# Weight sums of the layer 1 projection made one stage earlier, its products, slots and queues put in another order

## What is computed

```
z = h_lat @ w_in                               # 1024 x 1024 by 1024 x 2560
q = z[..., :o1]; k = z[..., o1:o2]; v = z[..., o2:o3]; g = z[..., o3:]
q = axial_rope(q, cos_r, sin_r, cos_c, sin_c)  # x*cos + swapped(x)*sin
k = axial_rope(k, cos_r, sin_r, cos_c, sin_c)
zc = h_ctx @ w_in[:, o1:o3]                    # context tokens: keys and values only
...                                            # windowed attention over q, k, v
y_lat = (o * jax.nn.silu(g)) @ w_out
```

## Time and profile before

| what | value |
|---|---|
| median of 3 runs | 1467.51 us |
| profiled execution, its own time | 1465.17 us |
| its span, first to last instruction | 1463.3 us |
| mean granted PE clock | 0.973 of full |
| PE busy | 1356.0 us (93%) |
| DVE busy | 974.8 us (67%) |
| ACT busy | 764.6 us (52%) |
| POOL busy | 558.1 us (38%) |
| layer 1's pairs, first to last matmul | 900.03 to 1126.56 us |

### The profile page before, as it was taken

The page is one execution under the profiler, slowest core; times in us unless marked ns, Lnnn a source line. Parts: engine busy times, 40 slices in busy tenths (PEclk is TensorE's granted clock), DMA queues, the critical chain, the costliest instruction groups (busy, mean ns, idle before and its releaser), DMA issues. The chain is left out here.

```text
span 1463.3 us, 20257 instructions
## 1 busy us (share of the span) xinstructions
PE 1356.0 (93%) x7116; PEld 1147.2 (78%) x7116; DVE 974.8 (67%) x1380; ACT 764.6 (52%) x1230; POOL 558.1 (38%) x297
## 2 busy tenths in 40 slices
PE   5999999999999999999999999578966899998898
PEld 4788888888888888878888887466755788887786
DVE  7788878777787878832111556777532899997742
ACT  5474838374656556832222434232421899997521
POOL 0024131322222323114434345576410666666642
PEclk9999999999999999999999999789987999999999
DMA  9413122212122222544344444434374744233683
GB/s 376 157 59 127 66 91 77 93 63 93 63 93 74 86 100 64 214 151 143 115 129 155 147 166 133 133 108 121 110 184 130 208 129 110 79 94 101 201 253 121
DMA packets 100894, 187.21 MB, mean 128 GB/s; under 512 B 11072, under 2 KB 59744, under 8 KB 98528
## 3 DMA queue, kind: packets, MB, share of 16 engines
q1 hardware_dynamic: 100832, 186.41, 39.8%
HBM read 137.08 MB, written 49.30 MB: 127 GB/s over the span
## 5 line engine op out<-in xcount | busy, mean ns | idle before, releaser
L1061 PE MATMUL slab<-h_hi,w_hi 128*128 128x512 f32 x720 | 256.3, 356 | 3.4 <-DVE h_lo L400 2.6
L1062 PE MATMUL slab<-h_lo,w_hi 128*128 128x512 f32 x720 | 255.6, 355 | 0.0
L1063 PE MATMUL slab<-h_hi,w_lo 128*128 128x512 f32 x720 | 255.1, 354 | 0.0
L1033 POOL TENSOR_TENSOR w_lo<-wraw,w_hi 128x1024 fp32r<-128x1024 f32 x29 | 78.5, 2706 | 300.5 <-ACT w_hi L653 300.5
L2792 POOL TENSOR_TENSOR probs<-probs,rdenom 128x2560 f32<-128x2560 f32 (+1 forms) x32 | 135.7, 4242 | 52.9 <-DVE rdenom L2740 52.9
L1061 PEld LDWEIGHTS slab<-h_hi,w_hi 128*128 128x128 f32 x720 | 136.5, 190 | 23.3 <-DVE h_lo L400 2.9
L1063 PEld LDWEIGHTS slab<-h_hi,w_lo 128*128 128x128 f32 x720 | 136.3, 189 | 19.2
L1062 PEld LDWEIGHTS slab<-h_lo,w_hi 128*128 128x128 f32 x720 | 136.5, 190 | 18.9
L2761 DVE TENSOR_TENSOR pt_lo<-TB,pt_hi 128x512 fp32r<-128x512 f32 x152 | 103.9, 687 | 26.9 <-ACT pt_hi L2700 24.7
L2732 DVE CUSTOM_DVE_ANT_0 probs<-S,mask,nsink 128x640 f32<-128x640 f32 (+1 forms) x128 | 107.6, 843 | 2.5 <-PE S L2823 2.3
L2661 ACT ACTIVATE probs<-probs,neg_max 128x640 f32<-128x640 f32 (+1 forms) x128 | 102.7, 802 | 11.9 <-DVE neg_max L2732 9.3
(11 more groups left out here) (409 smaller groups left out, 3584.2 us busy)
## 6 DMA issues: line engine op xcount, KB each, us to landing
wraw<-in_w_in SPq DMA_DIRECT2D x32, 512.0 KB, 3.5
wm<-in_wm SPq DMA_DIRECT2D x32, 512.0 KB, 3.7
mixT<-work SPq DMA_DIRECT2D x16, 640.0 KB, 4.0
wm<-in_wm SPq DMA_DIRECT2D x8, 1024.0 KB, 17.0
mraw<-mixT SPq DMA_DIRECT2D x16, 512.0 KB, 6.3
q_parts<-qT SPq DMA_DIRECT2D x32, 256.0 KB, 5.0
oT<-o_out SPq DMA_DIRECT2D x8, 1024.0 KB, 6.9
work<-in_xT SPq DMA_DIRECT2D x8, 640.0 KB, 8.4
```

Source lines behind the costliest of these rows:

```text
L1033: sub(w_lo[:, j % 2].rearrange("p k n -> p (k n)"), wraw[:, j % 2, :], v32(w_hi[:, j % 2].rearrange("p k n -> p (k n)")), ALU.subtract).th ...
L1061: nc.tensor.matmul(out, l_hi, r_hi, start=start, stop=False)
L1062: nc.tensor.matmul(out, l_hi, r_lo, start=False, stop=False)
L1063: return nc.tensor.matmul(out, l_lo, r_hi, start=False, stop=stop)
```

## The change

The weight sums leave the pairs. `weight_sums(n)` on DVE makes the four sums of pair n during tile n of layer 0's output projection: SP loads the pair's two slabs to `early` (`load_pair`, which waits until the sums of the pair before are stored), DVE runs four instructions of 128x512, and SP stores two slabs of sums to a new DRAM tensor `w_sum` (`store_sums`). The first loads of layer 1 now wait until the last sums have landed. Inside the pairs, SP loads the sums ready made: `load_s34` and `load_s21` (128x1024 each), `load_x` as before (A11, A12), `load_a22` half a slab. From pair 2 on they have four slots.

POOL keeps the sine products and nothing else: the token sums (16 instructions of 128x512) and the low parts of rotated keys and queries go to DVE. The product with the cosines is written to PSUM (`VP`) and no longer to SBUF, and so is the tanh of the gates. Query results have 8 slots, `q_hi` and `q_lo` 4 each; gate results have 8 slots (`RG` and `gates`).

PE's order is S1, S2, A12, S3, S4 of a pair, then A11 of the next, then A22 of this one. The other queues follow: the copies, rotations and stores of a pair's last halves come in the next pair's turn. Attention's load of the second query block waits for the even gate pairs' stores.

```diff
         w_hi, w_lo, c1 = laid_over(nc, ("w1_hi", [P, 2, KT, P], F32R), ("w1_lo", [P, 2, KT, P], F32R),
                                    ("h1_c1", [P, 2, 2, KH, 512], F32R))
-        wb4, wb6, wb5, C, Z, R4 = laid_over(
+        wb4, wb6, wb5, Z, RQ = laid_over(
             nc, ("w1_s3", block, F32R), ("w1_a22", block, F32R), ("w1_s4", block, F32R),
-            ("rope_cosined", [P, 2, 512], F32), ("rope_swap", [P, 2, 512], F32), ("q_halves", [P, 4, 512], F32))
+            ("rope_swap", [P, 2, 512], F32), ("q_halves", [P, 8, 512], F32))
...
-        _, TG = laid_over(nc, ("over_kv_rows_too", [P, 2 * T], F32), ("g_tanh", [P, 2, 512], F32))
+        _, wraw3, wraw2, _, RG = laid_over(
+            nc, ("below_first_q", [P, 256], F32), ("w1_raw3", [P, 512], F32), ("w1_raw2", [P, D], F32),
+            ("over_first_q", [P, 512], F32), ("g_halves", [P, 4, 512], F32))
         sb("over_gw_end_too", [P, 256])
...
+
+        def load_pair(n):
+            if isinstance(n, int) and n == 0:
+                low_ready(sp, K2 - 3)
+                low_ready(sp, K2 - 2)
+            else:
+                sp.wait_ge(wss.sem, wss.at + 32 * n)
+            for i in range(2):
+                sp.dma_start(early[:, i, :], a["w_in1"][2 * n + 4 + i]).then_inc(wsr.sem, 16)
+
+        def store_sums(n):
+            sp.wait_ge(ws.sem, ws.at + 4 * n + 4)
+            for i in range(2):
+                sp.dma_start(a["w_sum"][n, i], early[:, i + 1, :]).then_inc(wss.sem, 16)
 
         def load_w(i):
...
+                store_sums(KT - 1)
+                sp.wait_ge(wss.sem, wss.at + 32 * KT)
                 first_loads()
             load_x(t)
             if not (isinstance(t, int) and t >= TT - 2):
                 load_mix(t + 2, 0)
                 load_mix(t + 2, 1)
+            if not (isinstance(t, int) and t >= KT):
+                store_sums(t - 1)
+                load_pair(t)
             store(t - 1, 1 - s)
 
...
+        def weight_sums(n):
+            x1_, x2_ = early[:, 0, 0:512], early[:, 0, 512:D]
+            y1_, y2_ = early[:, 1, 0:512], early[:, 1, 512:D]
+            dve.wait_ge(wsr.sem, wsr.at + 32 * n + 32)
+            if isinstance(n, int) and n == 0:
+                low_ready(dve, K2 - 1)
+            tt(early[:, 2, 0:512], x1_, y1_, ALU.subtract).then_inc(ws.sem, 1)
+            dve.wait_ge(ws.sem, ws.at + 4 * n + 1)
+            tt(y1_, y2_, early[:, 2, 0:512], ALU.subtract).then_inc(ws.sem, 1)
+            dve.wait_ge(ws.sem, ws.at + 4 * n + 2)
+            tt(y2_, y1_, x1_, ALU.add).then_inc(ws.sem, 1)
+            tt(early[:, 2, 512:D], x2_, y1_, ALU.subtract).then_inc(ws.sem, 1)
+
         def body(t, s, last):
             if not last:
-                epilogue(t - 1, 1 - s)
+                if isinstance(t, int) and t < 4:
+                    epilogue(t - 1, 1 - s)
+                    weight_sums(t - 1)
+                else:
+                    weight_sums(t - 1)
+                    epilogue(t - 1, 1 - s)
...
+    def raw_block(p, i):
+
+        slot, part = {A11: (0, 0), A12: (0, 1), S2: (1, 0), S1: (1, 1), S3: (2 if p > 1 else 0, 0), S4: (2 if p > 1 else 0, 1), A22: (3 if p > 1 else 1, 0)}[i]
+        return wraw[slot][:, part * 512:part * 512 + 512].rearrange("p (k n) -> p k n", n=P)
 
     def banks(p):
...
     def result(k):
 
-        return home1.R4[:, k % 4, :] if k < 4 * Q_PAIRS else gates[:, k % 4, :]
+        if k < 4 * Q_PAIRS:
+            return home1.RQ[:, k % 8, :]
+        return (home1.RG[:], gates)[k // 4 % 2][:, k % 4, :]
 
     def rotated(n):
 
         if n < 2:
             return R_kv[n][:, 0:N_LAT], CK[:], ZK[:], cos, sin
         p, m, t = half_of(n - 2)
-        return result(n - 2), C[:, n % 2, :], Z[:, n % 2, :], cos[:, t * 512:(t + 1) * 512], sin[:, t * 512:(t + 1) * 512]
+        return result(n - 2), VP[:, n % 2, :], Z[:, n % 2, :], cos[:, t * 512:(t + 1) * 512], sin[:, t * 512:(t + 1) * 512]
...
+                sp.wait_ge(bl.sem, bl.at + place(p, A12))
+                sp.dma_start(wraw[0], a["w_sum"][p, 1]).then_inc(w_ld[0], 16)
+            else:
+                if p == 2:
+                    sp.wait_ge(kst.sem, kst.at + 64)
+                else:
+                    sp.wait_ge(bl.sem, bl.at + place(p - 1, S4))
+                sp.dma_start(wraw[2], a["w_sum"][p, 1]).then_inc(sums_ld.sem, 16)
+
+        def load_s21(p):
             if p == 0:
                 sp.wait_ge(wl[1].sem, wl[1].at + 2)
             else:
-                sp.wait_ge(bl.sem, bl.at + 7 * (p - 1) + A22 + 1)
-            sp.dma_start(wraw[1], a["w_in1"][5 + 2 * p]).then_inc(w_ld[1], 16)
+                sp.wait_ge(bl.sem, bl.at + place(p - 1, S2 if p > 2 else A22))
+            sp.dma_start(wraw[1], a["w_sum"][p, 0]).then_inc(w_ld[1], 16)
+
+        def load_a22(p):
+            if p < 2:
+                sp.wait_ge(bl.sem, bl.at + place(p, S2))
+                sp.dma_start(wraw[1][:, 0:512], a["w_in1"][5 + 2 * p, :, 512:D]).then_inc(w_ld[1], 16)
+            else:
+                if p == 2:
+                    sp.wait_ge(kst.sem, kst.at + 64)
+                else:
+                    sp.wait_ge(bl.sem, bl.at + place(p - 1, A22))
+                sp.dma_start(wraw[3], a["w_in1"][5 + 2 * p, :, 512:D]).then_inc(a22_ld.sem, 16)
 
         def store_v(n):
...
+        def take(k):
             p, j = k // 4, k % 4
-            act.wait_ge(pp.sem, pp.at + 7 * p + product)
+            act.wait_ge(pp.sem, pp.at + place(p, (A11, S1, S2, A22)[j]))
             if p < Q_PAIRS:
-                if p > 0:
-                    act.wait_ge(rl.sem, rl.at + k - 1)
+                if k >= 8:
+                    act.wait_ge(rl.sem, rl.at + k - 5)
             elif p == Q_PAIRS:
-                if j == 0:
-                    act.wait_ge(rs.sem, rs.at + 2 + 4 * Q_PAIRS)
-                    act.wait_ge(rc.sem, rc.at + 2 + 4 * Q_PAIRS)
+                act.wait_ge(kst.sem, kst.at + 64)
+            elif p == Q_PAIRS + 1:
+                act.wait_ge(rs.sem, rs.at + 2 + 4 * Q_PAIRS)
+                act.wait_ge(rc.sem, rc.at + 2 + 4 * Q_PAIRS)
             else:
-                act.wait_ge(gst[j // 2], 32 * (p - Q_PAIRS))
-            nc.scalar.activation(result(k), banks(p)[bank], ACT.Copy).then_inc(cp.sem, 1)
+                act.wait_ge(gst[p % 2], 64)
...
+        def add_product(k):
+            p, j = k // 4, k % 4
+            dve.wait_ge(pp.sem, pp.at + place(p, (A12, S3, S4)[j]))
+            dve.wait_ge(cp.sem, cp.at + copied(k))
+            tt(result(k), result(k), banks(p)[(2, 0, 1)[j]], ALU.add).then_inc(cs.sem, 1)
...
-            sines(0)
-            rotated_lo(0)
-            sines(1)
-            for p in range(PAIRS):
-                more = p + 1 < PAIRS
-                k = 4 * p
-                if p > 0:
-                    half_sines(k - 1)
-                    half_lo(k - 2)
-                    half_lo(k - 1)
-                if more:
-                    third_sum(p + 1)
-                if p == 0:
-                    second_sum(1)
-                    rotated_lo(1)
-                half_sines(k)
-                if more:
-                    if p > 0:
-                        second_sum(p + 1)
-                    first_sum(p + 1)
-                    fourth_sum(p + 1)
-                half_lo(k)
-                half_sines(k + 1)
-                half_sines(k + 2)
-                half_lo(k + 1)
+            for n in range(2 + 4 * Q_PAIRS):
+                sines(n)
 
         return split, rest
 
...
+        half(0, A11)
         for p in range(PAIRS):
-            for i in (A11, A12, S2, S1, S3, S4, A22):
+            if p > 0:
+                half(p - 1, A22)
+            for i in (S1, S2, A12, S3, S4):
                 half(p, i)
+            if p + 1 < PAIRS:
+                half(p + 1, A11)
+        half(PAIRS - 1, A22)
 
```

More of the change, by code:

```diff
@@ L1741, in projections1 @@
     Q_PAIRS = KT // 2
-    A11, A12, S2, S1, S3, S4, A22 = range(7)
+    A11, S1, S2, A12, S3, S4, A22 = range(7)
     HALVES = [(0, 0), (1, 1), (0, 1), (1, 0)]
     T_TILES = (2, 3, 0, 1)
-    KD_AT, QB_AT = 5, 6
+    T_ORDER = [0, 1, 2, 4, 5, 6, 3, *range(7, 16)]
     def kv_count(s, c):
@@ L1923, in rest @@
             load_x(0)
-            load_y(0)
+            load_s21(0)
             for n in range(4):
@@ L2074, in rest @@
             evict(1, 0)
-            for n in range(3):
+            for n in (0, 1, 2, 4, 5, 6):
                 t_hi(n)
@@ L2082, in rest @@
             value_hi(1)
+            block_hi(0, A11)
             evict(2, 2)
@@ L2085, in rest @@
             value_hi(3)
-            block_hi(0, A11)
-            block_hi(0, A12)
-            for n in range(3, 7):
-                t_hi(n)
+            t_hi(3)
             value_hi(4)
             t_hi(7)
-            block_hi(0, S2)
             evict(2, 0)
@@ L2105, in rest @@
             evict(3, 1)
-            block_hi(0, A22)
             for p in range(PAIRS):
@@ L2244, in rest @@
                 k = 4 * p
```

(25 more changed lines are left out.)

402 lines of the change are left out of this document (212 added, 190 removed).

## The result

| | before | after |
|---|---|---|
| median of the runs | 1467.45 us (4 runs, 1465.69 to 1468.35) | 1422.64 us (4 runs, 1420.79 to 1424.49) |
| ratio | | 0.9696, 95% interval 0.9679 to 0.9713 |
| profiled execution, its span | 1465.17, 1463.3 us | 1424.49, 1422.7 us |
| output projection, from its third tile to the first key product | 182.3 us | 201.9 us |
| first key product to first pair product | 62.7 us | 58.6 us |

The change makes the kernel 44.8 us faster. The forecast was 65, so the measured time lies above the forecast range. The pair stage came out nearly as worked out; the output projection of layer 0, which was priced at nothing, became 20 us longer.

The account below looks back on a forecast made before the run. Bound: layer 1's pairs, query pairs by a chain over POOL, gate pairs by result slots. 154.5 + 2 + 4.2 + 2 + 1.7 = 164.4 us for a stage of 229.7, so 1399.9 profiled, 1402 us median; range 1391 to 1419.

Parts of the forecast that it names:

- Sums in the output projection: Layer 0's output projection: the added DVE sums, loads and stores fit into free time, so they cost 0.
- Rival 4: Output projection: SP's round trip of the sums ahead of the `x1` store lengthens eight turns; 1470 us, chance 2%.
- Layer 1's first loads, "hidden": End of the output projection: these loads wait some 6 us for the last sums to land, hidden; uncovered 6 us.
- 56 products at full clock, 154.5 us: Layer 1's pair stage: PE must do 56 block products of 2.76 us each, 154.5 us.
- Query pairs: Layer 1's pairs 1 to 3: DVE sets 20.7 us a pair, 1.4 over PE's 19.3; 4.2 us (0 to 8).
- rival 1: Pairs 1 to 3: DVE's chain of waits, not its sum, sets 24 us a pair; +15, 1417 us, chance 14%.
- above 23 us: Sign in layer 1's pairs: the prediction is wrong if query pairs stay above 23 us.
- Gate pairs: Layer 1's gate pairs: with more result slots PE should run; gaps of 0.5 us a pair, 2 us (0 to 10).
- if ACT still waits for `sgT`: Sign in layer 1's gate pairs: the prediction is wrong if ACT still waits for `sgT` stores to land.
- Product order and lag: Layer 1's pairs: each PSUM bank gets at least one product, 2.76 us, before reuse; four waits a pair become none.
- Start-up: Pairs 0 and 1, which share slots and get sums late: 2 us (0 to 8), replacing gaps of 3.16 and 16.63.
- DVE with PSUM: Cosine product and tanh writing PSUM: 0 added per instruction, up to 0.9 us possible, four times a pair.

## Why the prediction was wrong, step by step

On the profiled execution the forecast was 1399.9 us and 1424.5 was measured, 24.6 more. The first pair product came at 917.1 and not at 896.9 (+20.2), the pair stage took 167.8 and not 164.4 (+3.4), and what follows 1.1 more.

*Sums in the output projection: the step that failed.* It compared SP's wait for "a landing of 6.3" with 14 us free ahead of the `x1` store, summed DVE's work against DVE's idle time, and came to "Price 0". Both sums were right as sums: the runs with the DMAs alone and with DVE's work alone cost 1 and 0 to 3 us, and DVE's work beside POOL took 7.4 us a turn where 7 was worked out. What it left out is that the two are joined. `weight_sums` is an instruction of DVE's fixed order with a wait in it, for a load that waits for a store that waits for the sums before; and from turn 4 the normalisation of the finished tile is queued behind it. The landing that counts is not one but two (8.7 and 6.7 us), and what waits for them is not only the `x1` store but everything on DVE. The question what is queued behind the waiting instruction was asked for SP only, and not for DVE. The runs show the price of the joined order: 18 us. Rival 4 had the place right and the mechanism wrong: it looked at SP, where the experiment with the DMAs alone shows that nothing is lost.

*Layer 1's first loads, "hidden".* In the changed kernel they came at 827.83, not at 796. In the kernels with the sums behind the epilogue they or the `x` load behind them cost 8 to 18 us, so a price of 6 for the uncovered case was too low. In the changed kernel itself this makes the stage's last wait of 2.72 us: `xt` is issued at 830.23, behind the first loads, and POOL waits 5.5 us for it.

*56 products at full clock, 154.5 us.* PE was busy 158.7 us, with two slow products: right.

*Query pairs.* 20.7 us each was forecast for pairs 1 to 3. From A22 to A22 they take 24.85, 23.61 and 20.26 us (963.59 - 938.74 and so on). So 6.6 us more in all; by the prediction's own mark, "above 23 us", the step is wrong for the first two. Their length is rival 1's, but not its mechanism in full: DVE waits 3.8 us for POOL's sines, not 8. Pair 3 has the forecast length, with DVE busy 18.86 of 20.26 us. That the excess of pairs 1 and 2 is start-up is shown for a part of pair 1 only, by the key's low part moved two instructions; for pair 2 it stays open.

*Gate pairs.* 2 us of gaps forecast; there is one of 0.59, and fewer slots bring one of 4.85 back. By the sign "if ACT still waits for `sgT`" the step is not clean: two waits of 3 us are left, but PE does not feel them.

*Product order and lag.* The four waits a pair were to become none. Three for ACT's copies (4.9 us) and two for DVE's low parts (2.7 us) are left in pairs 0 to 2, and three small ones of 1.4 us together (0.8 for DVE's sums, 0.6 for ACT's copy).

*Start-up.* 2 us forecast, 1.6 in pair 0 (1.01, 0.40, 0.22). Right, though what the start-up does to pairs 1 and 2 was counted elsewhere.

*DVE with PSUM.* 0 taken, 0 to 0.9 kept open: 692 and 682 ns. Right.

*Token sums on DVE, 0.* Keys and values take 58.6 us, and the first pair product follows without the old gap of 3.16. Right.

*Clock.* One fall of 1.65 us forecast; there are two in the pairs, behind gaps of 2.32 and 2.67 us. Two more in the output projection were not forecast: behind the wait of 8.0 (mean granted clock 0.91 and 0.97 in those two turns) and behind that of 2.72 (0.66 in the 4 us after it).

*A pair with all of POOL's disturbance.* The prediction makes three of them 1 us longer than with its 20.7. By its own terms such a pair is 15.9 + 5.1 + 0.7 = 21.7, so three are 3 us longer. Nothing else in the forecast uses the 1 us.

The 3.4 us by which the pair stage was missed are made of larger errors that partly cancel. The query pairs lost 10.8 us over PE's 57.9, clock falls included, where 5.9 was forecast; the gate pairs and the start-up lost 2.2 where 4 was forecast.

## What to carry to other kernels

Work that fits by its sum into idle engine time is free only if no wait comes with it, or if nothing that the busy engine needs is queued behind that wait. When work with a load of its own is put into a loop, follow the closed path (store, landing, load, landing, compute, the next store) through every engine's order, and compare its length with the turn. Put such work at the place where its engine must wait anyway: the same 32 instructions cost 18 us with 20 of them ahead of the epilogue, and 1 to 2 us between `xn` and `hb` with the `x` load out of their way.

An experiment that leaves the time unchanged can still have removed the cause: look where the gaps are before a theory is dropped.

## What was not expected of the hardware

All four sums have two SBUF inputs. In the run with DVE's sums alone one of them took 2332 ns on the mean of eight beside POOL, and 680 to 690 ns is what the sums take without it, so 3.4 times as long; the trace of before showed 1.53 beside 0.67 us. In the changed kernel's turn 3 one of them stands beside a POOL instruction of twice its size:

```profile
705.76 2.28 POOL L1644 TENSOR_TENSOR hb<-hb,mods 128x1024 f32<-128x1024 f32 x1 [10.09 <-DVE hb L1565]
...
706.32 2.27 DVE L1580 TENSOR_TENSOR early<-early 128x512 f32<-128x512 f32 x1
```

It starts 0.56 us into POOL's instruction and ends 0.55 us behind that one's end, about its own length. The Trainium skill (SBUF — State Buffer, section "Who interferes with whom") calls the port pair that the two engines share an exclusive lock. The trace agrees: the sum got through only when POOL's instruction was over.

In the changed kernel's pairs, gaps of 2.32 and 2.67 us were each followed by a product with a stretch at half clock (4.47 and 4.57 us in place of 2.88 from first start to last end), gaps of 1.25 us and less were not. Between the two the length of the gap does not settle it: behind 2.17 us, in the run with A22 first, the mean granted clock of the next 4 us was 0.65; behind 2.92 us, in the run with fewer slots, and behind 3.12 us, in the run with the DMAs alone, it stayed at 1.00.
